# Prompt attention on one core: the causal mask of the diagonal blocks, from a bf16 matmul on TensorE to an add on VectorE in PSUM

## What is computed

```python
Q_BLOCK = 128                       # S = 1024, so 8 query blocks
...
s = jnp.einsum('bqhl,bkl->bhqk', ql_b, c_kv) + jnp.einsum('bqhr,bkr->bhqk', qr_b, k_rope)
s = s.astype(jnp.float32) * ATTN_SCALE
q_pos = i * Q_BLOCK + jnp.arange(Q_BLOCK)
s = jnp.where(q_pos[:, None] >= k_pos[None, :], s, -jnp.inf)
p = jax.nn.softmax(s, axis=-1).astype(c_kv.dtype)
return jnp.einsum('bhqk,bkl->bqhl', p, c_kv)
```

## Time and profile before

| what | value |
|---|---|
| runs | 2021.01, 2023.7, 2024.94 us |
| median | 2023.7 us |
| the profiled execution's own time | 2023.47 us |
| its span in the profile | 2021.6 us |
| granted TensorE clock over the span, share of full speed | 0.994 |
| TensorE matmul busy | 97% of the span |
| TensorE weight load busy | 89% |
| VectorE busy | 65% |
| ScalarE busy | 42% |
| GpSimd busy | 45% |

### The profile page before, as it was taken

How to read it: one execution, slowest core, us unless ns; L and a number is a source line. 1 busy time by engine, 2 the same in 40 slices (tenths; PEclk the granted TensorE clock), 3 DMA queues, 4 the chain that set the end, 5 groups by cost and what they waited for, 6 DMA issues and landing times.

```text
span 2021.6 us, 34444 instructions
## 1 busy us (share of the span) xinstructions
PE 1962.3 (97%) x13460; PEld 1804.5 (89%) x13460; DVE 1304.2 (65%) x1714; ACT 845.2 (42%) x1451; POOL 908.6 (45%) x509
## 2 busy tenths in 40 slices
PE   8999999999999999989999999989999999899998
PEld 8999999999998998976669999989999999667886
DVE  3999999946745665644444315987777777537352
ACT  4222322315337767663351113843445444334342
POOL 4712344411211001124411245788787887467584
PEclk9999999999999999999999999999999999999999
DMA  6422223314420000155734332422222222656563
GB/s 219 151 92 74 95 85 97 103 64 175 143 91 23 16 7 23 56 200 216 282 146 149 126 115 75 138 64 87 73 85 75 85 75 94 208 176 238 153 225 113
DMA packets 190589, 238.12 MB, mean 118 GB/s; under 512 B 20573, under 2 KB 152175, under 8 KB 186333
## 3 DMA queue, kind: packets, MB, share of 16 engines
q1 hardware_dynamic: 172656, 163.42, 25.8%
q0 software_dynamic: 8320, 46.27, 5.9%
q10 hardware_dynamic: 9469, 26.36, 3.4%
HBM read 188.71 MB, written 48.15 MB: 117 GB/s over the span
## 4 chain that ended last, share of the span: by engine, by line
PE 85%; DVE 7%; ACT 3%; issue 2%; DMA 2%; POOL 1%; ACTq 0%; DVEq 0%; SPq 0%
PE ps L2507 32%; PE ps L3162 14%; PE ps L2700 9%; PE ps L3229 9%; PE pst L3162 5%; PE pst L3229 3%; PE ps L2914 2%; PE pst L2779 1%; PE ps L2967 1%; PE pst L2946 1%; DMA inr<-f_d 1%; DVE tfr L2338 1%; PE ps L2768 1%; PE ps L2766 1%; PE pst L2949 1%
## 5 line engine op out<-in xcount | busy, mean ns | idle before, releaser
L1580 POOL TENSOR_TENSOR wlo<-wraw,whi 128x1024 fp32r<-128x1024 f32 x66 | 160.4, 2435 | 386.8 <-ACT whi L879 291.9
L1847 DVE SCALAR_TENSOR_TENSOR pst<-g_ext,wtap,pst 128x512 f32<-128x512 f32 x464 | 306.9, 746 | 0.0
L2507 PE MATMUL ps<-xh,whi 128*128 128x352 f32 x864 | 187.2, 325 | 1.2 <-ACT stat L973 1.2
L2507 PE MATMUL ps<-xh,wlo 128*128 128x352 f32 x864 | 186.3, 323 | 0.0
L2507 PE MATMUL ps<-xl,whi 128*128 128x352 f32 x864 | 186.1, 324 | 0.0
L2399 DVE TENSOR_TENSOR x1l<-inr,x1h 128x384 fp32r<-128x384 f32 (+1 forms) x66 | 87.8, 1354 | 100.1 <-ACT x1h L1470 100.0
L2507 PEld LDWEIGHTS ps<-xh,whi 128*128 128x128 f32 x864 | 147.0, 189 | 1.9 <-issue 1.8
L2507 PEld LDWEIGHTS ps<-xh,wlo 128*128 128x128 f32 x864 | 148.4, 188 | 0.0
L2507 PEld LDWEIGHTS ps<-xl,whi 128*128 128x128 f32 x864 | 146.7, 188 | 0.0
L1780 POOL TENSOR_TENSOR wlo<-pieces,whi 128x1024 fp32r<-128x1024 f32 x44 | 109.7, 2498 | 78.0 <-ACT whi L1462 77.9
L1656 POOL TENSOR_TENSOR wlo<-wraw,whi 128x1024 fp32r<-128x1024 f32 (+1 forms) x12 | 24.2, 2028 | 246.5 <-ACT whi L1057 246.5
(11 more groups left out here) (492 smaller groups left out, 5604.7 us busy)
## 6 DMA issues: line engine op xcount, KB each, us to landing
pieces<-in_w_down SPq DMA_DIRECT2D x44, 512.0 KB, 4.7
wraw<-in_w_in SPq DMA_DIRECT2D x37, 512.0 KB, 3.8
f_d<-hv SPq DMA_DIRECT2D x22, 528.0 KB, 2.7
wraw<-in_w_down SPq DMA_DIRECT2D x22, 512.0 KB, 4.4
wraw<-in_w_up SPq DMA_DIRECT2D x40, 256.0 KB, 3.8
x1f<-in_w_up SPq DMA_DIRECT2D x40, 256.0 KB, 3.9
inr<-f_d SPq DMA_DIRECT2D x44, 192.0 KB, 2.4
xt_d<-tmp POOLq DMA_DIRECT2D x8, 528.0 KB, 3.5
```

Of the source, the lines that this page charges most:

```text
L1580: nc.gpsimd.tensor_tensor(wlo[:, n % HL, :], wraw[:, n % RAW, :], whi[:, n % HL, :].bitcast(F32), ALU.subtract).then_inc(lo_done, 1)
L1847: half[x] = link(nc.vector.scalar_tensor_tensor(out=dst, in0=src, scalar=tap(k_), in1=pst[:, x, :], op0=ALU.mult, op1=ALU.add))
L2507: last = nc.tensor.matmul(out[:, c, 0:CH], w[:, k, :], x[:, k, c * CH:(c + 1) * CH], start=(k == 0 and x is hi_x and w is wh), stop=(k == ...
```

## The change

TensorE no longer adds the mask. VectorE adds the fp32 mask into the last 128 columns of the scores, in place in PSUM, right ahead of the row maximum, and the maximum waits for that add by a new semaphore `mask_done`. That holds for every block of every head: 64 matmuls with their weight loads go, 64 adds of 128 x 128 and 64 waits come. The two bf16 copies on ScalarE go, with their wait for the mask's load; VectorE gets that wait ahead of its first work for the attention. No other instruction is moved.

```diff
-        maskb = at("maskb", [P, P], BF16, 3648)
-        identb = at("identb", [P, P], BF16, 3904)
...
+        mask_done = sem("scores_masked")
...
-            act.wait_ge(c2_in, 16)
-            nc.scalar.activation(maskb[:, :], maskc[:, :], ACT.Copy)
-            nc.scalar.activation(identb[:, :], ident[:, :], ACT.Copy)
...
             def dve_max(h, i):
                 dve.wait_ge(s_done, 8 * h + (i + 1))
+                c, n = len(key_parts(i)) - 1, key_parts(i)[-1][1] - key_parts(i)[-1][0]
+                diag = psx[i % 2][:, c, n - P:n]
+                nc.vector.tensor_tensor(diag, diag, maskc[:, :], ALU.add).then_inc(mask_done, 1)
+                dve.wait_ge(mask_done, 8 * h + (i + 1))
                 nc.vector.reduce_max(nmx[:, i:i + 1], score_block(i), axis=AX.XY if i == 4 else AX.X, negate=True
                                      ).then_inc(mx_done, 1)
...
             dve.sem_inc(pt_lo, 2)
+            dve.wait_ge(c2_in, 16)
             dve_project(0, 0, "rope", 0)
...
                     nc.tensor.matmul(out, qr2[:, cols], kr2[:, ks], start=False, stop=False)
-                    diag = k1 == (i + 1) * P
-                    last = nc.tensor.matmul(out, qr2[:, cols], krl[:, ks], start=False, stop=not diag)
-                    if diag:
-                        last = nc.tensor.matmul(psx[q][:, c, n - P:n], identb[:, :], maskb[:, :],
-                                                start=False, stop=True)
+                    last = nc.tensor.matmul(out, qr2[:, cols], krl[:, ks], start=False, stop=True)
                 last.then_inc(s_done, 1)
```

## The result

The changed kernel takes 2032.89 us (median of 6 runs, 2028.79 to 2034.78), the kernel before 2022.62 us in the 6 runs taken with it (2019.06 to 2024.94). The two medians differ by 10.3 us; the ratio on record is 1.0045, with a 95% interval of 1.0034 to 1.0055, which is 9.1 us slower, between 6.9 and 11.1. The change is a loss, a little larger than the 7.6 us of the forecast. The profiled execution took 2028.79 us, for a span of 2027.0; it is the fastest of the six.

A forecast was written before the change was run, and what follows sets the result against it. TensorE has almost no room, but its waits end chains through row maxima, where the add lies. Odd heads 2.58, head 7 1.15, even heads 2.70, head 6 1.20: 7.6 us slower, 2023.47 + 7.6 = 2031.1 us, range 2024.5 to 2035.

The forecast's parts named there:

- b: Price of one add where VectorE stands waiting for TensorE: the maximum starts 0.29 us later, saved matmul already taken off.
- Rival 2: VectorE's wait on its own semaphore is free, the maximum overlapping the add: +4.2 us, 2027.6 us; chance 0.14.
- The chain in odd heads: Heads 1, 3, 5: delays at scores 2, scores 4 and transposes 4, 2b + a - 0.07 = 0.86 us per head.
- a: Price of one add where VectorE comes late from other work: the maximum starts 0.35 us later.
- Head 7: Casts no weights, so block 4's add is bare too: 3b + a - 0.07 = 1.15 us longer.
- The even heads: Heads 0, 2, 4: 0.40 us lost at transposes 0, 0.64 at transposes 4, less twice 0.07: 0.90 us each.
- blocks 5 to 7 have projections behind them on TensorE as cover: Adds of the last blocks cost TensorE nothing; if that fails, transposes 5 are the next to be late.
- Rival 3: TensorE's time is all that counts, every add is covered: 4.5 us saved, 2019.0 us; chance 0.05.
- Rival 1: Even heads hide their adds and only odd heads pay: +1.5 us, 2025.0 us; chance 0.12.
- rival 4: The add in place in PSUM is dear, 0.60 us each: +16.0 us, 2039.5 us; chance 0.09.
- rival 5: The clock falls in the longer waits of the heads: above 2040 us; chance 0.02.
- To the end: Behind the attention stage: the whole delay of 7.6 us reaches the end of the span.

The follow-up runs named there:

- runs 9: Kernel before with the add on VectorE for block 6 alone, matmuls for the other seven blocks: ratio 1.0001 (0.999 to 1.0011).
- 11: Kernel before with the add on VectorE for block 7 alone, matmuls for the other blocks: ratio 0.9994 (0.9984 to 1.0004).
- Run 6: Kernel before with the add on VectorE for blocks 0, 1, 2, 4 and 5, the matmul for 3, 6 and 7: ratio 1.0031 (1.002 to 1.0042).
- run 10: Kernel before with the add on VectorE for block 3 alone, matmuls for the other blocks: ratio 0.9994 (0.9983 to 1.0005).
- filled kernel: Changed kernel with eight extra unused matmuls in TensorE's gap ahead of scores 2 of head 0: ratio 1.0032 (1.0021 to 1.0042) against the kernel before.
- runs 5: Kernel before with the add on VectorE for blocks 3, 6 and 7, matmuls for the other blocks: ratio 1.0006 (0.9997 to 1.0016).
- run 4: Kernel before with the mask's matmul removed and nothing put in its place: ratio 0.9991 (0.9981 to 1.0).
- run 7: Changed kernel with the add made twice for each maximum, each with its own wait: ratio 1.0111 (1.0094 to 1.0128) against the kernel before.
- run 3: Changed kernel with the mask's matmul kept beside the add on VectorE: ratio 1.0056 (1.004 to 1.0071) against the kernel before.

## Why the prediction was right, and where it was off

**The prices.** The add took 0.281 to 0.300 us over its 64 instances, where I had taken 0.31 between 0.279 and 0.341. Its row in the groups by line and shape of the changed kernel:

```profile
L2025 DVE TENSOR_TENSOR ps<-ps,maskc 128x128 f32<-128x128 f32 x64 | 18.9, 295 | 23.5 <-PE ps L2768 22.7
```

The maximum starts 0.03 us behind its add: 644.84 + 0.30 = 645.14, next start 645.17; it is 34 or 35 ns in all 64 places. So b is: L2768 of scores 2 ends at 646.90 + 0.34 = 647.24, the maximum starts at 647.61, 0.37 us behind, where it was 0.10: 0.27 us instead of the 0.29 of the forecast. Rival 2, the free wait, falls with that row: the maximum doesn't overlap the add, while the reciprocal behind it starts at 648.09, before the maximum's end at 648.17, as it did in the earlier trace rows. The Trainium skill, "VectorE: DVE Perf Modes", section "The DRAIN you can't avoid", says of a series of copies that the semaphore costs nothing extra; these rows don't bear that out for an add and the maximum that waits for it. No run leaves out the wait, so its price is that of these two pairs of instructions and not of the same pair with and without.

**Two readings of the kernel before.** The stretches of the earlier trace rows were not cut at the heads: from score to score odd head 1 is 35.40 us long and even head 2 36.10, with TensorE idle for 0.60 and 0.06 us. And the wait of 0.32 us ahead of scores 4 is that of the weight load (PEld); the matmuls stood still for 0.08 us there. 0.24 + 0.08 + 0.28 is the 0.60. The argument that odd heads have room and even ones almost none stands.

**The chain in odd heads** came out in size: 0.78 to 0.80 us against 0.86, with b and a a little smaller. Its way was in part another, as "Hidden adds" tells. Head 7 came out at 1.10 against 1.15.

**The even heads** came out right by errors that cancelled. Both places that I named lose time. Matmul by matmul against the first trace, head 2 loses 0.51 us at scores 2 and behind transposes 0 and 0.73 at transposes 4, and masks 0 to 5 give 0.43 back; 0.81 us together, where my terms of the same places make 0.97 (0.40 - 0.07 + 0.64). At the first place the wait begins at scores 2 and not at transposes 0, and scale 0 is late by 0.53 us and not by 2a = 0.70. Two things I had not seen: transposes 5 give 0.22 us back, since the wait ahead of them is taken up by that at transposes 4, and transposes 7 come 0.32 us late. That makes 0.91 us, measured 0.94, forecast 0.90. The step that fails is "blocks 5 to 7 have projections behind them on TensorE as cover": alone, add 6 costs an even head 0.21 to 0.28 us and add 7 0.14 to 0.20 (runs 9 and 11). Transposes 7 wait for the low half of block 6 at the end of VectorE's list in an even head. It stands behind the rotary and key work for the next head (L1997 now, L2001 before), for which VectorE waits on ScalarE, and ScalarE comes to that from block 7. By the clock of the span the rotary step moved from 704.36 to 708.84 us, by 4.48, where transposes 5 moved from 698.41 to 702.51, by 4.10. VectorE and TensorE in the changed kernel:

```profile
711.26 1.15 DVE L2039 TENSOR_TENSOR ptl<-pst,pth 128x512 fp32r<-128x512 f32 x2
```

```profile
712.09 0.52 PE L2776 MATMUL pst<-ident,pbuf 128*128 128x128 f32 x3 [0.16 <-DVE ptl L2039]
```

**Hidden adds.** Of add 3 I said nothing, and so had it at nothing. That was wrong: in the changed kernel it lies on the path that sets ScalarE's casts in an odd head. I had ScalarE late by 2b through maximum 2. In head 1 scale 2 waits 0.15 us for the reciprocal behind maximum 3, and ScalarE is late by 0.45 us from there on: b from add 0, 0.07 back for mask 2, b from add 3. Add 4 is hidden behind the casts, as said, but only just: the reciprocal behind it ends at 652.40, scale 3 starts at 652.50.

```profile
649.85 0.62 ACT L1171 ACTIVATE pbuf<-pbuf,rinv 128x384 f32<-128x384 f32 x1 [0.15 <-DVE rinv L2032]
...
652.25 0.15 DVE L2032 RECIPROCAL rinv<-rs 128x1 f32<-128x1 f32 x1
...
652.50 0.71 ACT L1171 ACTIVATE pbuf<-pbuf,rinv 128x512 f32<-128x512 f32 x1
```

Run 6 has no add 3. There scale 2 waits for nothing and is late by 0.21 us, and scale 3 is late by 0.42 us: the casts end at 650.52, the reciprocal behind add 4 at 650.61, and scale 3 starts 0.04 us behind the reciprocal.

```profile
647.79 0.61 ACT L1177 ACTIVATE pbuf<-pbuf,rinv 128x384 f32<-128x384 f32 x1
...
649.90 0.62 ACT L1064 ACTIVATE whi<-wraw 128x512 fp32r<-128x512 f32 x1
...
650.46 0.15 DVE L2040 RECIPROCAL rinv<-rs 128x1 f32<-128x1 f32 x1
...
650.65 0.72 ACT L1177 ACTIVATE pbuf<-pbuf,rinv 128x512 f32<-128x512 f32 x1
```

So the odd heads are late by the same 0.77 to 0.80 us with add 3 and without, since the path through add 4 is as long; alone add 3 costs its full 0.26 us (run 10). That my sum had the size right with add 3 left out is luck. What an add of 0.3 us costs alone and what it adds to the sum are two questions.

**TensorE's saving.** Rival 3 falls: with no mask at all heads 1 to 7 gain 2.02 us, and the matmuls kept beside the adds cost 1.9 us more. Rival 1 falls with the even heads, which became longer, and rival 4 with the add's 0.295 us.

**The clock**, rival 5, was put at a chance of 0.02 and at over 2040 us. Its mechanism came true in one place, at a smaller price. I had argued from gaps of 0.3 us in heads 1 and 2 that new gaps would stay below 1 us, and had not looked at head 0, where there was a gap of 1.57 us already. That is the step that made the forecast small: 1.24 us. The filled kernel's stage, +7.60, is the forecast's 7.6.

**To the end.** I let the delay reach the end whole. Matmul by matmul, the changed kernel's first trace stays 9.45 us behind that of the kernel before (0.5 us of it from ahead of the stage) from the end of the stage up to 1717 us, with changes of 0.1 us at most but for 0.4 us near 1336 us, given back at once; so the step holds that far. Then it drops to 5.4: 2.2 us with the wait for rr's load, which this trace lacks, and 1.6 us with a clock drop behind that wait, which it lacks too. The second trace has that wait. It stays 10.5 us behind (1.5 from ahead of the stage) and drops to 8.2, mostly at a wait of TensorE for the low half of weights from GpSimd, 2.20 us where it was 4.48. So single traces took a part of the delay back, but not in a way that follows the stage: behind it, the two traces of the kernel before and runs 5, 9, 10 and 11 took 1149.0 to 1150.9 us, the seven others 1145.7 to 1150.7. Among these are run 4, whose stage is shorter than before, with 1146.5, and run 7, whose stage is the longest, with 1150.7. The medians show no such gain: 9.1 us (6.9 to 11.1) and, the second time, 0.0057 x 2023.26 = 11.5 us (8.9 to 14.4) for a stage of 8.8. Whether the shorter rest of these traces has a cause, and what made the second ratio larger than the stage, stays open.

## What to carry to other kernels

A busy share of 97% on one engine doesn't say that its instructions set the end: look at what ends its waits, and where a chain through other engines does, the busy engine can be the better place for a cheap operation. Here a matmul that cost TensorE 0.07 us at most was better than an add of 0.30 us on VectorE ahead of its reduction. Price such an edit per place: the new operation and its handover where the engine stood waiting, room first where it came late, and the saved time only where no new wait eats it. Before calling an add hidden, follow each of its readers to the next wait, and ask which path takes over when it is gone. Look also at the gaps that are already long, for they may become clock drops.

## What the runs showed of the hardware that was not expected

In head 0 a gap of 2.10 us between matmuls was followed by 3.4 us at a granted clock of 0.51, in both traces of the changed kernel; a gap of 1.57 us was not, in the kernel before; filled up to 0.32 us it was not either. All thirteen traces fall in line: the gap was 1.55 to 1.57 us in six (the kernel before twice, runs 5, 9, 10 and 11), with no drop, and 1.78 (run 4), 1.88 (run 3), 2.10 to 2.11 (the changed kernel twice, run 6) and 2.44 us (run 7), with a drop each time. They all share one place in one program: the runs don't separate the length of the gap from what TensorE did ahead of it and when. Removing the matmul without any add set the drop off as well, and made the first head 1.25 us longer: less work for the bounding engine made its stretch slower.
